# Front of a mixer and expert block: low parts on VectorE, gates as tanh, an undivided softmax, heads kept in PSUM

## The reference, cut to what matters

```python
h = rmsnorm(x, mix_norm_g);  proj = h @ w_in           # u_pool | q | k | v | gate logits
gates = sigmoid(proj[..., o_g:] + b_branch_gate)       # g_pool, g_attn
y_pool = (group_map(trailing_mean(u) - u) * pool_scale) @ pool_up
q, k = rotary(rmsnorm(q, q_norm_g)), rotary(rmsnorm(k, k_norm_g))
sc = (q . k) * HEAD_DIM ** -0.5, masked by chunks of 64
p = softmax(sc);  a = p[:, :, 0] - lam * p[:, :, 1]    # two maps per head
o = rmsnorm(a @ v, subln_g) * (1 - lam_init)           # per head of 128
y_attn = o @ attn_up
x = x + (g_pool * y_pool + g_attn * y_attn) @ w_out
x = x + moe_ffn(rmsnorm(x, ffn_norm_g))                # top 4 of 32, SwiGLU experts of 1024
```

## Time and profile before

| what | us |
|---|---|
| median of three runs | 1133.53 |
| the three runs | 1127.86 to 1135.07 |
| the profiled execution | 1134.66 |
| its span (first to last instruction) | 1132.4 |
| TensorE busy in the span | 1094.2 |
| VectorE, ScalarE, GpSimd busy | 293.9, 190.8, 62.6 |

### The profile page before, as it was taken

One profiled execution on the slowest core, in us unless ns is written; L12 is line 12 of the kernel. 1 busy time (PEld: TensorE's weight loads), 2 busy tenths in 40 slices (PEclk: granted clock), 3 DMA queues, 4 the chain that ended last, 5 costly groups with the idle time before them and its releaser, 6 DMA issues.

```text
span 1132.4 us, 13271 instructions
## 1 busy us (share of the span) xinstructions
PE 1094.2 (97%) x5385; PEld 468.4 (41%) x5385; DVE 293.9 (26%) x632; ACT 190.8 (17%) x361; POOL 62.6 (6%) x58
## 2 busy tenths in 40 slices
PE   7988998999999999999999999999999999999998
PEld 3787996333333333333333333333333333333332
DVE  4978564311111111111111111111111111111112
ACT  4645542000010001000100010001000100010000
POOL 0294220000000000000000000000000000000000
PEclk9998999899999999999999999999999999999999
DMA  9722468699999999999999999999999999999995
GB/s 325 264 76 112 149 257 336 278 417 422 428 427 430 428 428 427 431 427 429 428 429 427 429 431 427 427 429 430 427 427 430 431 427 426 432 429 427 427 431 221
DMA packets 43486, 432.55 MB, mean 382 GB/s; under 512 B 5829, under 2 KB 6378, under 8 KB 18890
## 3 DMA queue, kind: packets, MB, share of 16 engines
q1 hardware_dynamic: 42906, 431.60, 91.0%
q10 hardware_dynamic: 560, 0.68, 0.2%
HBM read 431.22 MB, written 1.05 MB: 382 GB/s over the span
## 4 chain that ended last, share of the span: by engine, by line
PE 84%; DVE 11%; ACT 2%; SPq 1%; issue 1%; DMA 1%; DVEq 0%; ACTq 0%
PE ps L754 58%; PE ps L761 8%; PE ps L726 6%; PE ps L719 3%; DVE arena L1332 3%; PE ps L492 2%; PE ps L494 2%; PE ps L493 2%; DVE arena L1330 2%; DVE ring_r L1074 1%; DMA ring<-in_w_in 1%; SPq L436 1%; ACT ring_r L815 1%; PE ps L779 1%; DVE arena L1143 1%
## 5 line engine op out<-in xcount | busy, mean ns | idle before, releaser
L754 PE MATMUL ps<-ring,arena 128*64 128x512 f32 x3072 | 676.3, 593 | 0.0
L754 PEld LDWEIGHTS ps<-ring,arena 128*64 128x64 f32 x3072 | 220.7, 137 | 440.2 <-issue 440.2
L1320 DVE TENSOR_SCALAR arena<-ps 128x512 f32<-128x512 f32 x32 | 22.1, 692 | 474.7 <-PE ps L754 474.7
L761 PE MATMUL ps<-arena 128*64 128x512 f32 x384 | 102.9, 614 | 1.2 <-issue 0.4
L1330 DVE TENSOR_SCALAR arena<-ps 128x512 f32<-128x512 f32 x32 | 22.1, 692 | 235.5 <-PE ps L754 235.5
L972 ACT COPY arena<-ps 128x512 f32<-128x512 f32 x32 | 18.8, 587 | 325.0 <-PE ps L713 325.0
L726 PE MATMUL ps<-arena 64*128 64x512 f32 x264 | 65.6, 615 | 0.8 <-ACT arena L978 0.8
L713 PE MATMUL ps<-arena 128*64 128x512 f32 x264 | 64.0, 607 | 0.8 <-DVE arena L1265 0.8
L492 PE MATMUL ps<-ring_r 128*128 128x256 f32 (+1 forms) x192 | 61.6, 321 | 2.8 <-DVE ring_r L1074 2.4
L970 ACT ACTIVATE arena<-arena 128x512 f32<-128x512 f32 x32 | 20.1, 629 | 244.9 <-DVE arena L1320 244.9
L978 ACT COPY arena<-ps 128x512 f32<-128x512 f32 x32 | 18.8, 586 | 248.8 <-PE ps L754 248.8
(11 more groups left out here) (185 smaller groups left out, 655.0 us busy)
## 6 DMA issues: line engine op xcount, KB each, us to landing
ring<-in_exp_w_gate SPq DMA_DIRECT2D x64, 2048.0 KB, 19.5
ring<-in_exp_w_up SPq DMA_DIRECT2D x64, 2048.0 KB, 21.7
ring<-in_exp_w_down SPq DMA_DIRECT2D x64, 2048.0 KB, 21.7
ring<-in_w_in SPq DMA_DIRECT2D x8, 2048.0 KB, 8.6
ring<-in_w_out SPq DMA_DIRECT2D x2, 2048.0 KB, 7.8
xt<-in_x SPq DMA_DIRECT2D x4, 512.0 KB, 6.7
ring<-in_pool_up SPq DMA_DIRECT2D x1, 2048.0 KB, 7.2
ring<-in_attn_up SPq DMA_DIRECT2D x1, 2048.0 KB, 8.5
```

Of the source, the lines that this page charges most:

```text
L754: last = mm(ps[BLOCK * half:BLOCK * (half + 1), bank, :], src[:, c, k % 2, :], slot(n)[:, c, HALF * half:HALF * (half + 1)], start=False, ...
L761: mm(ps[BLOCK * half:BLOCK * (half + 1), bank, :], this_e[:, buf, k, :], bias_rows[:, HALF * half:HALF * (half + 1)], start=True, stop=False)
```

## The change

- All low parts are made by DVE. Those of GA_P, GA_P+1, PUP_P and the first quarter of GB_P are interleaved with the attention steps (`behind`): two quarters before step 0, two behind the difference in steps 0 to 2, one in steps 3 to 7. The other three quarters of GB_P come after the head sums of the second token block and before the merges of pool_up. GpSimd keeps the pooling, the low parts of the merged stream and some fills.
- Every gate is tanh(x/2 + b/2) on ACT; the merge computes (tanh + 1) times the strip in one instruction (twice the sigmoid), and the halves go into `phalf` (the pooling scale) and `subln8` (the head norm's gain). `sigmoid_rest` is gone.
- 1/8 is multiplied into the query gain `gq` once; the maximum is negated in its reduction, so L1136 is gone.
- The softmax of a head is left undivided: with sums d0 and d1, DVE forms ratio = -lambda d0/d1 and the difference e0 + ratio e1, which is d0 times the old one. The head norm takes d0 squared times EPS in place of EPS (`oeps`), which gives the same normalised head.
- The products of a token block's four heads go side by side into PSUM bank 3, and PE waits once (at the fifth unit) for the block to be read. ACT squares all four heads in one instruction (`head_squares`), DVE sums them (`head_sums`); the first block is copied to SBUF, the second is normalised straight from PSUM.

```diff
 SPLIT = [K_P, V_P, U_P, GA_P, GA_P + 1, PUP_P, GB_P, GB_P + 1, AUP_P, WO_P, WO_P + 1]
-BY_GPSIMD = (GA_P, GA_P + 1, PUP_P, GB_P)
...
 def lo_count(n, q):
-    if n in BY_GPSIMD:
-        return w_lo_pool, PARTS * BY_GPSIMD.index(n) + q + 1
-    return w_lo, PARTS * [k for k in SPLIT if k not in BY_GPSIMD].index(n) + q + 1
+    return PARTS * SPLIT.index(n) + q + 1
...
 STEPS_ATT = len(units) + 2
-LATE = 3
...
         pe.wait_ge(w_hi, PARTS * SPLIT.index(n) + q + 1)
-        pe.wait_ge(*lo_count(n, q))
+        pe.wait_ge(w_lo, lo_count(n, q))
...
                 strip_read(pe, ("qkv", 5))
-            if step >= 3:
-                pe.wait_ge(o_ready, step - 2)
+            if step - 2 == HEADS:
+                pe.wait_ge(o_ready, 1)
             for kc in range(t + 1):
-                last = mm(ps[:, 3, 0:VD], diffT[:, step % 2, P * kc:P * (kc + 1)],
+                last = mm(ps[:, 3, VD * h:VD * (h + 1)], diffT[:, step % 2, P * kc:P * (kc + 1)],
                           vtok[:, kc, VD * h:VD * (h + 1)], start=(kc == 0), stop=(kc == t))
...
-    def gate_e(c):
+    def gate_tanh(c):
         s = ("gate", c)
         strip_wait(act, s)
-        strip_release(fn(gate[:, c, :], strip_bank(s)[:, 0:S], ACT.Exp, bias=ngate[:, c:c + 1], scale=-1.0), s)
-    def gate_sigmoid(c):
-        s = ("gate", c)
-        strip_wait(act, s)
-        strip_release(fn(gate[:, c, :], strip_bank(s)[:, 0:S], ACT.Sigmoid, bias=bgate[:, c:c + 1]), s)
+        strip_release(fn(gate[:, c, :], strip_bank(s)[:, 0:S], ACT.Tanh, bias=hgate[:, c:c + 1], scale=0.5), s)
...
                 last = fn(y_split[0][:, 2 * i + g, :], strip_bank(s)[:, S * g:S * (g + 1)], ACT.Copy,
-                          scale=cols[:, R_PSCALE + 2 * i + g:R_PSCALE + 2 * i + g + 1])
+                          scale=phalf[:, 2 * i + g:2 * i + g + 1])
             last.then_inc(y_hi, 1)
...
     ahead += [[(PUP_P, q)] for q in range(PARTS)] + [[(GB_P, 0)], [], [(GB_P, 1)], [(GB_P, 2), (GB_P, 3)]]
-    fill = ([lambda: u_copy(2), lambda: u_copy(3)] + [lambda c=c: gate_e(c) for c in range(NC - LATE)]
-            + [lambda c=c: gate_sigmoid(c) for c in range(NC - LATE, NC)])
+    fill = [lambda: u_copy(2), lambda: u_copy(3)] + [lambda c=c: gate_tanh(c) for c in range(NC)]
+    def head_squares(t):
+        act.wait_ge(o_done, HEADS * (t + 1))
+        if t == 0:
+            nc.scalar.copy(otok[:, t, :], ps[:, 3, :])
+        fn(junk[:, t, 0:HALF], ps[:, 3, :], ACT.Square).then_inc(o_ready, 1)
     for step in range(STEPS_ATT):
...
                 fn(prob[:, b, m, 0:keys], ps[:, 4 + 2 * b + m, 0:keys], ACT.Exp, bias=mx[:, b, m:m + 1],
-                   scale=HD ** -0.5, accum_out=den[:, b, m:m + 1]).then_inc(exp_ready, 1)
+                   accum_out=den[:, step, m:m + 1]).then_inc(exp_ready, 1)
         fill[step]()
...
             nc.scalar.copy(diffT[:, (step - 1) % 2, 0:P * (t + 1)], ps[:, 2, 0:P * (t + 1)]).then_inc(diffT_ready, 1)
-        if step >= 2:
-            t, h = units[step - 2]
-            act.wait_ge(o_done, step - 1)
-            nc.scalar.copy(otok[:, t, VD * h:VD * (h + 1)], ps[:, 3, 0:VD])
-            fn(junk_o[:], ps[:, 3, 0:VD], ACT.Square, accum_out=oss[:, step - 2:step - 1]).then_inc(o_ready, 1)
+        if step - 1 == HEADS:
+            head_squares(0)
         for n, q in ahead[step]:
             hi_part(n, q)
+    head_squares(1)
     act.wait_ge(o_var, 1)
...
     for c in range(NC, NC + 4):
-        gate_sigmoid(c)
+        gate_tanh(c)
     for t in range(NT):
...
     for c in range(NC + 4, 2 * NC):
-        gate_sigmoid(c)
+        gate_tanh(c)
     hi_parts(WO_P + 1)
...
-    def lo_parts(n):
-        hi, lo = split_piece(n)
-        for q in range(PARTS):
-            pool.wait_ge(w_hi, PARTS * SPLIT.index(n) + q + 1)
-            gp.tensor_tensor(quarter(lo, q), quarter(ring[:, n % LAND, :], q), quarter(hi, q).bitcast(F32),
-                             ALU.subtract).then_inc(w_lo_pool, 1)
-    lo_parts(BY_GPSIMD[0])
     for g in range(NG):
-        if g == NG // 2:
-            lo_parts(BY_GPSIMD[1])
         strip_read(pool, ("u", g))
...
         gp.tensor_tensor(pT[:, g, :], pT[:, g, :], uT[:, g, PAD:], ALU.subtract).then_inc(pooled, 1)
-    for n in BY_GPSIMD[2:]:
-        lo_parts(n)
     for m in range(NC):
...
     dve.wait_ge(cols_ready, 1)
-    v.tensor_scalar(ngate, cols[:, R_BGATE:R_BGATE + 2 * NC], -1.0, None, ALU.mult)
-    own(v.tensor_scalar(subln8, cols[:, R_SUBLN:R_SUBLN + 1], 1.0 - LAM_INIT, None, ALU.mult))
+    v.tensor_scalar(hgate, cols[:, R_BGATE:R_BGATE + 2 * NC], 0.5, None, ALU.mult)
+    v.tensor_scalar(phalf, cols[:, R_PSCALE:R_PSCALE + NG], 0.5, None, ALU.mult)
+    own(v.tensor_scalar(subln8, cols[:, R_SUBLN:R_SUBLN + 1], 0.5 * (1.0 - LAM_INIT), None, ALU.mult))
...
     dve.wait_ge(par_in, 16 * PARAMS)
+    v.tensor_scalar(gq, gq, HD ** -0.5, None, ALU.mult)
     own(v.tensor_tensor(lamv[:, 0:2, :], lamv[:, 0:2, :], lamv[:, 2:4, :], ALU.mult))
...
-    def sigmoid_rest(c):
-        strip_read(dve, ("gate", c))
-        own(v.tensor_scalar(gate[:, c, :], gate[:, c, :], 1.0, None, ALU.add))
-        return v.reciprocal(gate[:, c, :], gate[:, c, :])
+    def head_sums(t):
+        dve.wait_ge(o_ready, t + 1)
+        return v.tensor_reduce(oss[:, HEADS * t:HEADS * (t + 1)],
+                               junk[:, t, 0:HALF].rearrange("p (h d) -> p h d", h=HEADS), AX.X, ALU.add)
+    lo_part(GA_P, 0)
+    lo_part(GA_P, 1)
+    behind = [[(GA_P, 2), (GA_P, 3)], [(GA_P + 1, 0), (GA_P + 1, 1)], [(GA_P + 1, 2), (GA_P + 1, 3)]]
+    behind += [[(PUP_P, q)] for q in range(PARTS)] + [[(GB_P, 0)]]
     for step in range(len(units)):
...
         dve.wait_ge(scored, step + 1)
-        own(v.tensor_reduce(mx[:, b, :], ps[:, 4 + 2 * b:6 + 2 * b, 0:keys], AX.X, ALU.max))
-        v.tensor_scalar(mx[:, b, :], mx[:, b, :], -HD ** -0.5, None, ALU.mult).then_inc(max_ready, 1)
-        if step >= LATE:
-            own(sigmoid_rest(step - LATE))
+        v.tensor_reduce(mx[:, b, :], ps[:, 4 + 2 * b:6 + 2 * b, 0:keys], AX.X, ALU.max,
+                        negate=True).then_inc(max_ready, 1)
         dve.wait_ge(exp_ready, 2 * step + 2)
-        own(v.reciprocal(den[:, b, :], den[:, b, :]))
-        own(v.tensor_tensor(den[:, b, 1:2], den[:, b, 1:2], neglam, ALU.mult))
-        own(v.tensor_scalar(prob[:, b, 1, 0:keys], prob[:, b, 1, 0:keys], den[:, b, 1:2], None, ALU.mult))
-        v.scalar_tensor_tensor(out=diff[:, b, 0:keys], in0=prob[:, b, 0, 0:keys], scalar=den[:, b, 0:1],
-                               in1=prob[:, b, 1, 0:keys], op0=ALU.mult, op1=ALU.add).then_inc(diff_ready, 1)
+        own(v.reciprocal(rden[:, step:step + 1], den[:, step, 1:2]))
+        own(v.scalar_tensor_tensor(out=ratio[:, step:step + 1], in0=den[:, step, 0:1], scalar=neglam,
+                                   in1=rden[:, step:step + 1], op0=ALU.mult, op1=ALU.mult))
+        v.scalar_tensor_tensor(out=diff[:, b, 0:keys], in0=prob[:, b, 1, 0:keys], scalar=ratio[:, step:step + 1],
+                               in1=prob[:, b, 0, 0:keys], op0=ALU.mult, op1=ALU.add).then_inc(diff_ready, 1)
+        for n, q in behind[step]:
+            lo_part(n, q)
+    head_sums(0)
+    v.scalar_tensor_tensor(out=oeps, in0=den[:, :, 0], scalar=EPS, in1=den[:, :, 0], op0=ALU.mult, op1=ALU.mult)
     for i in range(2):
...
             last = v.scalar_tensor_tensor(out=y_split[1][:, k, :], in0=strip_bank(s)[:, S * g:S * (g + 1)],
-                                          scalar=cols[:, R_PSCALE + k:R_PSCALE + k + 1],
+                                          scalar=phalf[:, k:k + 1],
                                           in1=y_split[0][:, k, :].bitcast(F32), op0=ALU.mult, op1=ALU.subtract)
...
-    dve.wait_ge(o_ready, len(units))
-    v.tensor_scalar(ors, oss, 1.0 / VD, EPS, ALU.mult, ALU.add).then_inc(o_var, 1)
+    own(head_sums(1))
+    v.scalar_tensor_tensor(out=ors, in0=oss, scalar=1.0 / VD, in1=oeps, op0=ALU.mult, op1=ALU.add).then_inc(o_var, 1)
+    for q in range(1, PARTS):
+        lo_part(GB_P, q)
...
             z = otok[:, t, :].rearrange("p (h d) -> p h d", h=HEADS)
-            v.tensor_tensor(z, z, wide(ors[:, HEADS * t:HEADS * (t + 1)], [P, HEADS, VD], 2),
+            full = ps[:, 3, :].rearrange("p (h d) -> p h d", h=HEADS) if t else z
+            v.tensor_tensor(z, full, wide(ors[:, HEADS * t:HEADS * (t + 1)], [P, HEADS, VD], 2),
                             ALU.mult).then_inc(o_normed, 1)
...
         strip_wait(dve, s)
-        if m >= NC - LATE:
-            strip_read(dve, ("gate", m))
-        strip_release(v.tensor_tensor(gate[:, m, :], strip_bank(s)[:, 0:S], gate[:, m, :], ALU.mult), s)
+        strip_read(dve, ("gate", m))
+        strip_release(v.scalar_tensor_tensor(out=gate[:, m, :], in0=gate[:, m, :], scalar=1.0,
+                                             in1=strip_bank(s)[:, 0:S], op0=ALU.add, op1=ALU.mult), s)
         if m == 1:
...
         strip_read(dve, ("gate", NC + m))
```

(14 more changed lines are left out.)

## The result

The changed kernel takes 1120.22 us (four runs, 1119.68 to 1121.32) against 1134.24 for the kernel before (1127.86 to 1135.07), 14.0 us faster by the medians, where 11 were forecast. The ratio, in which the one run of 1127.86 counts too, is 0.9892 with a 95% interval of 0.9874 to 0.9910: 12.2 us (10.2 to 14.3). The profiled execution took 1120.66 us with a span of 1118.9, 13.5 us less than before.

What follows compares the result with a forecast made beforehand. PE was taken to bound the kernel, with 20.9 us recoverable in the front; less 0.7, 2.2, 4.6 and 2.6 this left a gain of 10.8 us, so 1123 us as a median, range 1117 to 1130.

Steps and rivals of the forecast that it cites:

- stream rival: Late in the expert loop, the stream of 2 MB pieces sets the end and gives the gain back: about 1133; chance 0.04.
- old waits and low stretches: PE between 50 and 143 us: 12.4 us of waits for DVE plus 8.5 us of slow clock, 20.9 us recoverable.
- U_P's low part, group banks and the like: Waits of PE that remain: 0.4 us for the third input piece's low part, 0.3 us for the group banks' release.
- holds by pooling: Before step 3's difference, GpSimd's pooling holds 17 DVE instructions: 4.9 us less 2.7 slack, 2.2 us of PE time.
- third strip of pool_up: PE stands from 3.2 to 7.8 us after gate 7's strip, until DVE frees the first up-projection strip: 4.6 us.
- clock in 50 to 143 us: New stalls bring stretches at the lower PE clock: 2.6 us taken, ends 1.7 and 5.1.
- router and start of the loop: Behind the front: stages keep their order, no PE wait there for what the change moves; no term in the sum.
- clean pass: Rival: PE is not held by pooling and there is one low clock stretch: 1119.6 us; chance 0.20.
- Fourth, why DVE is late: Attention front: DVE's low parts and scalings last about as long as the GpSimd instruction beside them; 1.16 us when POOL rests.
- table load: Rival: Exp and Tanh tables alternate on ACT in each attention step, 6.4 us lost: 1129; chance 0.04.
- rule on the shared pair of ports: Two-input VectorE and GpSimd alternate by whole instructions; at its strictest (full turns) 9.2 us of stalls, 1132; chance 0.09.
- slower rival: Steps 0 to 3: VectorE is the bound, each low part pays 2.2 us, 14.9 us of stalls: 1138; chance 0.05.

Runs made afterwards that it cites:

- e8: Changed kernel with the pooling's arithmetic left out, GpSimd writing zeros in its place: 1119.60 us.
- e1: Changed kernel with the low parts of GA_P, GA_P+1, PUP_P and GB_P back on GpSimd: 1119.66 us.
- e3: Changed kernel with the last three low parts of GB_P made after the merges of strips 2, 3 and 4 of pool_up: 1116.06 us.
- e2: Kernel before with only the low parts moved from GpSimd to VectorE, interleaved as in the changed kernel: 1123.18 us.
- e4: Kernel before with only the gates as tanh, so no gate reciprocals on VectorE: 1130.04 us.
- e9: Kernel before with only the negated maximum (gq scaled once, L1136 gone): 1131.09 us.
- e11: Changed kernel with two products of one column, results unused, added to each step's chain: 1124.62 us.
- e5: Kernel before with only the undivided softmax, negated maximum included: 1122.57 us.
- e6: Kernel before with only the heads kept in PSUM: 1131.93 us.
- e10: e1 with two products of one column, results unused, added to each step's chain: 1127.64 us.
- e12: e3 with ScalarE's square of the second token block ahead of its last two high parts of GB_P: 1115.72 us.
- e7: e3 with 12 more 512-column matmuls of zeros while PE waits for the router's choice: 1115.64 us.

## Why the prediction was right, and where its sizes were off

**The end follows the front.** The head transposes start at 130.4 us and not 142.1, 11.7 us earlier; the loop's first product 12.7 us; the end 13.5. The expert stream gave nothing back: late in the loop a piece lands 31.8 us after its issue, as in the earlier trace rows. The stream rival falls. The median, 1120.2 us, lies inside the range and 2.8 us below the 1123 that was said.

**The terms.** The old waits and low stretches, 20.9 us with the clock, went as forecast. What was set against them:

| term | forecast | measured |
|---|---|---|
| U_P's low part, group banks and the like | 0.7 | 0.5 |
| holds by pooling | 2.2 | 0.7 |
| third strip of pool_up | 4.6 | 4.3 |
| clock in 50 to 143 us | 2.6 | 2.9 |
| router and start of the loop | 0 | -1.8 |

The first four leave 12.5 us, of which 11.7 had arrived at the head transposes; the 0.8 between is in no term and stays open. The mis-sized term is the pooling's. The forecast had 4.9 us of holds on 17 instructions, 0.39 each for three quarters of them. In the trace five of the eight low parts were held by 0.44 us (three not at all), three of the four combinations by 0.34 to 0.52, the ratios by 0.1 on average: 3.8 us, against a slack that the forecast had put at 2.7. VectorE finished the difference of step 3 at 77.1 us, where 73.6 was added up without holds, and PE asked for it at 76.4 (76.3 forecast). The wait that was left is 0.7 us, and by e8 that is its whole price. Of the rivals, the time of the clean pass (1119.6) was nearest to the measured, though not by its mechanism alone: the span fell 2.7 us more than the 10.8 of the sum, made up mainly of 1.5 in the pooling's term and 1.8 in the next one, which was luck, less the 0.8 that stays open.

**The term that was missing.** The forecast carried nothing behind the front. In the kernel before, the clock was low through the loop's first product; in the changed one it had come back before it. The tables by stretch, before and after:

```profile
204.00:209.00 5.00, 4.56 (x14) 1.85 (x15) 0.69 (x1) 1.28 (x1) 0.00 (x0) 0.50 0.02 7
```

```profile
192.00:200.00 8.00, 6.98 (x34) 3.05 (x36) 0.69 (x1) 1.44 (x2) 0.00 (x0) 1.00 0.22 50
```

From the head transposes to the loop's first product it is 65.2 us before and 64.2 in the changed kernel, and 0.8 us more is won in the loop's first microseconds: 1.8 us (13.5 - 11.7) that no edit of the change touches. In e1 and e3, where the clock comes back only after the first product has begun, the same stretch is 65.0 us long. The lower level around the router lasted 13.7 us before and in e1, e2, e3, e4, e9 and e11, 6.8 us in the changed kernel and in e5, e6, e8, e10 and e12, and 10.2 us in e7. From the head transposes to the end it is 989.5 to 990.3 us in the first group and 988.2 to 988.5 in the second. e3 and e12, which differ only in the place of one square well ahead of the head transposes, fall on different sides. No run shows what decides it; one profile against another can be off by 1 to 2 us for this reason alone.

**The step of the argument that failed** is not in the sum, but in "Fourth, why DVE is late". It named the holds as the cause and GpSimd's low parts as the thing to move. e1 shows that moving them as the change does was not needed once the chain is short, and e5 that the undivided softmax alone brings 10.7 us. The move is not worthless: with its own new wait at pool_up taken away, e3 is 3.6 us below e1.

The edits alone bring 10.0 (low parts), 10.7 (softmax), 3.2 (tanh) and 1.3 (heads, not told from none), 25 together against 14 measured for all (24 against 12 by the ratios). About 4 of the missing 11 us are the new wait at pool_up, which e3 removes; the rest is that the edits buy the same waits.

The account that these runs bear out: VectorE's step is its list plus its holds, and it is the long steps that make PE wait, not the average. In the kernel before, VectorE's longest step is 10.1 us against PE's 4.5, and PE then waits 4.6; in e4, where the gates are gone and the holds are not, it is 9.8 us, and PE waits 2.6; in e5 it is 7.3 us (its last), and PE waits 1.6. In e2 the list is too long almost without holds, 5.2 us. e1 still has a step of 7.2 us, and its difference comes less than 0.1 us before PE takes it: there the room won before it was just enough. e10 is the test from the other side: lengthened again by two instructions that can be held, e1 loses 6.6 us in these steps.

**The other rivals.** No table load stands between exponentials and tanh in the changed kernel's steps; with that the Trainium skill (ScalarE: Activation LUTs, "Table sets: the hidden batching unit") agrees, and the rival falls. The Trainium skill's rule on the shared pair of ports (SBUF — State Buffer, "SBUF: two separate sides") holds for single instructions, 2.58 us in e1 for one of 0.48, but as a price for PE it misled, since most holds fell into VectorE's slack. The slower rival needed holds of 1.65 us on each low part; it was 0.44 at most.

## What to carry to other kernels

A held or long instruction costs only where the step of its engine, list and holds together, exceeds the step of the engine that is fed by more than the room won before it. Price that sum step by step and not on average, and expect edits that shorten the same step not to add up. When work moves to another engine, look at the place where a wait is followed by moved work and then by the release that the bounding engine needs: three low parts ahead of the merges cost here 4 us of the 18 there were to win. When two variants are compared by one profile each, compare them between marks inside the stretch that was edited: here the clock moved the rest by up to 2 us.

## What was not expected of the hardware

Two instructions of one column, 0.2 us each, cost 6.6 us in eight steps beside GpSimd's 2.4 us instructions, and 1.5 us without them. With the hold going both ways, the pooling's additions on GpSimd rose from 0.64 to 1.13 us when VectorE had the low parts. And a wait's length alone does not tell what the clock adds: the same 2.4 us for the fourth low part of U_P stands before and in e1, with a granted clock of 0.89 from 50 to 65 us in the one and of 1.00 in the other; e10, the same program as e1 up to there, has 0.89. The row of e1:

```profile
50.00:65.00 15.00, 12.63 (x104) 11.67 (x103) 10.47 (x12) 10.07 (x19) 13.65 (x9) 1.00 0.37 141
```

After such a wait the forecast should leave about 1.7 us open (half of the 3.3 us that the lower level lasted before).
